# Two hybrid mixers on one core: decayed queries moved to VectorE, the triangular systems solved ahead of the index scores, gate panels fetched early, logarithms ahead of copies

## What is computed

```
n = rms_norm(h, norm_mix);  proj = n @ w_in
o_a = gated_deltanet(aq, ak, av, az, aa, ab)      # 4 heads of 128, chunks of 64
o_b = dsa_attention(bq, bk, bv, iq, ik, iw)       # index scores choose 64 of the keys per query
y = sigmoid(n @ w_gate + b_gate) gates (o_a @ w_a, o_b @ w_b);  h += y @ w_out
h += conv_gated_mlp(rms_norm(h, norm_ffn))
```

```
q, k = l2_norm(silu(conv(q))) * d**-0.5, l2_norm(silu(conv(k)))
g = -exp(a_log) * softplus(a + dt_bias);  gcum = cumsum(g);  decay = exp(gcum_i - gcum_j), i >= j
m = beta * (k k^T) * decay, strictly lower;  (m + I) [u, w] = [beta v, beta k exp(gcum)]
o = (q * exp(gcum)) S + ((q k^T) * decay) v_new     # S is the state carried from chunk to chunk
```

## Time and profile before

| | |
|---|---|
| median of three runs | 1621.33 us |
| profiled execution: its own time / its span | 1624.33 / 1622.5 us |
| TensorE matmul busy | 1583.8 us, 98% of the span |
| VectorE / ScalarE / GpSimd busy | 1178.0 (73%) / 904.1 (56%) / 71.1 us (4%) |
| mean granted TensorE clock | 0.991 |
| mixer of layer 0 / of layer 1 (from the index key's panel to the last gate panel) | 77.8 to 225 / 535 to 678 us |
| a gate load of 512 KB, from issue to landing, median | 4.4 us |

### The profile page before, as it was taken

One profiled execution on the slowest core, in us unless ns is written; L12 is line 12 of the kernel. 1 busy time (PEld: TensorE's weight loads), 2 busy tenths in 40 slices (PEclk: granted clock), 3 DMA queues, 4 the chain that ended last, 5 costly groups with the idle time before them and its releaser, 6 DMA issues.

```text
span 1622.5 us, 34719 instructions
## 1 busy us (share of the span) xinstructions
PE 1583.8 (98%) x12673; PEld 1546.3 (95%) x12673; DVE 1178.0 (73%) x1929; ACT 904.1 (56%) x1419; POOL 71.1 (4%) x62
## 2 busy tenths in 40 slices
PE   8998999999999989999999999999999999999998
PEld 7988989999999879899999989999999999999998
DVE  7778877766559689787665667888756746678863
ACT  5664565655546745656554555666545455566642
POOL 3111001000000101000000000000000000000000
PEclk9998999999999989999999999999999999999999
DMA  6633335555555432365656544566656535646553
GB/s 204 208 103 99 105 116 170 165 182 171 175 163 163 138 103 92 114 191 183 209 182 190 166 155 145 154 196 185 190 183 189 171 119 156 182 152 197 183 184 113
DMA packets 272207, 261.41 MB, mean 161 GB/s; under 512 B 20009, under 2 KB 270533, under 8 KB 272115
## 3 DMA queue, kind: packets, MB, share of 16 engines
q1 hardware_dynamic: 270547, 256.15, 50.9%
q0 software_dynamic: 1376, 3.87, 0.8%
q10 hardware_dynamic: 192, 0.14, 0.0%
HBM read 256.70 MB, written 3.42 MB: 160 GB/s over the span
## 4 chain that ended last, share of the span: by engine, by line
PE 81%; DVE 11%; ACT 4%; issue 2%; DMA 2%; SPq 1%; DVEq 0%; ACTq 0%
PE lin L551 22%; PE lin L554 22%; PE lin L559 22%; PE aux L899 5%; PE lin L899 3%; PE lin L605 3%; DVE wL L538 2%; PE lin L576 1%; ACT wH L529 1%; DVE cT L2075 1%; DMA stage<-in_w_gate 1%; DVE nT L2530 1%; DVE nT L2026 1%; DVE nL L2535 1%; PE lin L636 1%
## 5 line engine op out<-in xcount | busy, mean ns | idle before, releaser
L529 ACT ACTIVATE wH<-stage 128x1024 fp32r<-128x1024 f32 x488 | 493.7, 1049 | 481.9 <-PE lin L554 333.9
L538 DVE TENSOR_TENSOR wL<-stage,wH 128x1024 fp32r<-128x1024 f32 x488 | 580.1, 1231 | 142.2 <-PE lin L559 85.7
L551 PE MATMUL lin<-nH,wH 128*128 128x256 f32 (+2 forms) x2256 | 559.8, 287 | 1.4 <-DVE u L2579 0.7
L554 PE MATMUL lin<-nL,wH 128*128 128x256 f32 (+2 forms) x2256 | 554.7, 285 | 0.0
L551 PEld LDWEIGHTS lin<-nH,wH 128*128 128x128 f32 x2256 | 425.5, 189 | 4.7 <-issue 2.2
L554 PEld LDWEIGHTS lin<-nL,wH 128*128 128x128 f32 x2256 | 426.6, 189 | 1.1 <-issue 0.7
L559 PE MATMUL lin<-nH,wL 128*128 128x256 f32 (+2 forms) x2256 | 295.0, 283 | 0.6 <-DVE wL L538 0.6
L559 PEld LDWEIGHTS lin<-nH,wL 128*128 128x128 f32 x2256 | 281.4, 188 | 1.1 <-DVE wL L538 1.1
L551 PE MATMUL lin<-aH,wH 128*128 128x256 f32 (+1 forms) x704 | 172.3, 284 | 0.0
L554 PE MATMUL lin<-aL,wH 128*128 128x256 f32 (+1 forms) x704 | 172.2, 284 | 0.0
L551 PEld LDWEIGHTS lin<-aH,wH 128*128 128x128 f32 x704 | 132.8, 189 | 0.0
(11 more groups left out here) (416 smaller groups left out, 2202.4 us busy)
## 6 DMA issues: line engine op xcount, KB each, us to landing
stage<-in_w_up SPq DMA_DIRECT2D x88, 512.0 KB, 4.7
stage<-in_ffn_w_up SPq DMA_DIRECT2D x88, 512.0 KB, 4.1
stage<-in_w_in SPq DMA_DIRECT2D x52, 512.0 KB, 4.8
stage<-in_w_down SPq DMA_DIRECT2D x40, 512.0 KB, 3.7
stage<-in_ffn_w_down SPq DMA_DIRECT2D x40, 512.0 KB, 4.2
stage<-in_w_gate SPq DMA_DIRECT2D x32, 512.0 KB, 4.4
stage<-in_even_w_in SPq DMA_DIRECT2D x24, 512.0 KB, 4.6
stage<-in_w_out SPq DMA_DIRECT2D x16, 512.0 KB, 4.1
```

The lines of the kernel that those rows point to most:

```text
L529: nc.scalar.activation(wH[:, s, ks, 0:n], stage[:, s, ks, 0:n], ACT.Copy).then_inc(sem["whi"], 1)
L538: nc.vector.tensor_tensor(wL[:, s, ks, 0:n], stage[:, s, ks, 0:n], wH[:, s, ks, 0:n].bitcast(F32), ALU.subtract).then_inc(sem["wlo"], 1)
L551: mm = nc.tensor.matmul(banks[b][0:rows_, 0:width], wH[:, s, k, cols], xh, start=start and n == 0, stop=False)
L554: mm = nc.tensor.matmul(banks[b][0:rows_, 0:width], wH[:, s, k, cols], xl, start=False, stop=False)
```

## The change

The results are the same; the work of the two mixers is placed differently, on one engine also taken from another. VectorE's `decays(b)` is cut in two: `decay_logs(b)`, up to the release of the bank of gb, and `decays(b)`, from the wait for `dec` on. On TensorE the wait for `qe` is that of `delta_out`, on ScalarE the change of buffers is in `index_relu`, and the softplus functions moved up are those that stood behind the last norm logarithm; `w_in(6)` of ScalarE is written out so that the decay exponentials of block 2 come between its split and its copies. The diff, cut to its core:

```diff
@@ SyncE
                 gate(0, 0)
-                gate(0, 1)
                 for b in range(2):
                     kept_off(b)
+                gate(0, 1)
...
                 gate(1, 0)
+                gate(1, 1)
...
                 sp.wait_ge(sem["solved"], at("solved", l, 1))
...
                     sp.dma_start(A[b], by_token(za[b], b)).then_inc(sem["a_back"], 16)
-                gate(1, 1)
@@ GpSimd
-                    if n == 2:
-                        pool.wait_ge(sem["eg"], at("eg", l, 4))
-                        pool.wait_ge(*full("qk2", l))
-                        nc.gpsimd.tensor_tensor(cT[:, 0:4, :], cT[:, 0:4, :], eg[:, :, :], ALU.mult).then_inc(sem["qe"], 1)
@@ TensorE
-                turned("ta", iab, IDX_DIM, 16, lin_read[0])
+                turned("ta", iab, IDX_DIM, 16, (sem["iab"], at("iab", l, 1)))
...
                 index_products(1)
+                gate(0, [1])
                 pe.wait_ge(sem["sq_att"], at("sq_att", l, 1))
                 for h, name in enumerate([f"sbq{h}" for h in range(4)] + ["sbk"]):
                     mm(begin(name, l)[:, 0:T], ones, sq_att[:, h, :]).then_inc(filled(name), 1)
-                gate(0, [1])
...
-                    pe.wait_ge(sem["qe"], at("qe", l, 1))
+                    if b:
+                        pe.wait_ge(sem["qe"], at("qe", l, 1))
@@ ScalarE
+                split_hi(act, m0 + 5, 0, n=NARROW)
                 for s in range(2):
-                    split_hi(act, m0 + 5, s, n=PANEL if s else NARROW)
...
-                f(iab[IDX_DIM:NARROW, :], lin[0][IDX_DIM:NARROW, 0:T], Copy)
+                f(iab[IDX_DIM:NARROW, :], lin[0][IDX_DIM:NARROW, 0:T], Copy).then_inc(sem["iab"], 1)
+                root_log([f"ssq{h}" for h in range(4)], rnq, 1.0)
+                turned("ta", ab, 16)
+                split_hi(act, m0 + 5, 1)
+                act.wait_ge(sem["sp_in"], at("sp_in", l, 1))
+                own.done(f(gl[:, :, :], gm[:, :, :], Exp))
+                own.wait()
+                f(gl[:, :, :], gl[:, :, :], Ln, bias=one_col)
+                f(bt[:, :, :], ab[:, :, 12:16], Exp, scale=-1.0).then_inc(sem["sp_ln"], 1)
                 for p0 in (0, IDX_DIM):
                     t = f(ikr[p0:p0 + IDX_DIM, :], lin[0][0:IDX_DIM, 0:T], Copy)
...
                 f(sq_ik[:, :], ikr[:, :], Square).then_inc(sem["sq_ik"], 1)
-                root_log([f"ssq{h}" for h in range(4)], rnq, 1.0)
-                turned("ta", ab, 16)
                 root_log([f"ssk{h}" for h in range(4)], rnk, 1.0)
                 root_log(["sik"], rni, 1.0 / P)
-                act.wait_ge(sem["sp_in"], at("sp_in", l, 1))
...
-                w_in(6, lambda b: rawT[:, 16 + b:17 + b, :], slots=(0,))
+                split_hi(act, m0 + 7, 0)
                 decays(2)
+                act.wait_ge(sem["panel_done"], 2 * (m0 + 6) + 3)
+                for b in range(2):
+                    f(rawT[:, 16 + b:17 + b, :], lin[b][:, 0:T].unsqueeze(1), Copy).then_inc(lin_read[b], 1)
...
-                        if j and e < 2:
-                            act.wait_ge(sem["score"], at("score", l, e + 1))
-                        f(rl[:, e, :], bank(name)[:, :], Relu).then_inc(emptied(name), 1)
+                        if e >= 2:
+                            act.wait_ge(sem["score"], at("score", l, e - 1))
+                        f(rl[:, (2 * j + e) % 4, :], bank(name)[:, :], Relu).then_inc(emptied(name), 1)
...
                 index_relu(1)
+                gate_hi(0, [1])
                 root_log([f"sbq{h}" for h in range(4)] + ["sbk"], rnb, 1.0 / P)
                 root("sbk", rnb, 0.0)
-                gate_hi(0, [1])
@@ VectorE
                 split_lo(dve, m0 + 5, 0, NARROW)
                 times_sin(0, iq_s[:, :, :])
-                split_lo(dve, m0 + 5, 1)
                 added(0, rawT[:, 20:24, META:T], iq_s[:, :, :])
...
+                split_lo(dve, m0 + 5, 1)
...
+                decay_logs(0)
                 decays(0)
+                decay_logs(1)
                 decays(1)
...
                 keys_and_queries(1)
+                decay_logs(2)
                 times_sin(1, ik_s[:, :].unsqueeze(1))
                 decays(2)
...
                 split_lo(dve, m0 + M_GATE, 1)
+                solved()
                 index_scores(0)
-                solved()
                 gate_lo(0, [0])
                 dve.wait_ge(*read("qk2", l))
                 masked(4)
                 index_scores(1)
+                keys_decayed()
...
+                joined(4)
+                split_lo(dve, m0 + M_GATE + 1, 0)
+                masked(5)
                 take_eight(1)
-                keys_decayed()
-                split_lo(dve, m0 + M_GATE + 1, 0)
-                joined(4)
-                masked(5)
                 gate_lo(0, [1])
+                split_lo(dve, m0 + M_GATE + 1, 1)
                 dve.wait_ge(sem["att_unit"], at("att_unit", l, 3))
                 crossed(bk_s[:, :].unsqueeze(1), keys)
                 crossed(tmp4[:, :, :], queries)
-                split_lo(dve, m0 + M_GATE + 1, 1)
...
                 greatest(0)
                 biased()
+                v.tensor_tensor(cT[:, 0:4, :], cT[:, 0:4, :], eg[:, :, :], ALU.mult).then_inc(sem["qe"], 1)
                 gate_lo(2, [0])
                 normed(0)
                 state(0)
```

More of the change, by code:

```diff
@@ L211 @@
     "panel_in": 16 * M_LAYER, "whi": 4 * M_LAYER, "wlo": 4 * M_LAYER, "whi_used": 2 * M_LAYER, "panel_done": 2 * M_LAYER,
-    "lin_read": R_LAYER, "ab_in": 16,
+    "lin_read": R_LAYER, "ab_in": 16, "iab": 1,
     "sq": DC, "rstd": 2, "n": 2 * DC, "nh": DC, "nl": DC,
@@ L971, in head_squares, with turned @@
                         mm(begin(name, l)[:, 0:T], ones, sqh[:, h, :]).then_inc(filled(name), 1)
-                def turned(name, x, p0, n, free):
+                def turned(name, x, p0, n, there):
                     ps = begin(name, l)
-                    pe.wait_ge(free, r0 + 6)
+                    pe.wait_ge(*there)
                     for b in range(3):
@@ L992, in layer @@
                 t.then_inc(filled("gc"), 1)
-                turned("tv", bvT, 0, P, lin_read[3])
+                turned("tv", bvT, 0, P, (lin_read[3], r0 + 6))
                 def gate(i, slots=(0, 1)):
@@ L1558, in layer, with turned @@
                 act.wait_ge(sem["panel_done"], 2 * (m0 + 5) + 3)
-                f(iab[IDX_DIM:NARROW, :], lin[0][IDX_DIM:NARROW, 0:T], Copy)
+                f(iab[IDX_DIM:NARROW, :], lin[0][IDX_DIM:NARROW, 0:T], Copy).then_inc(sem["iab"], 1)
+                root_log([f"ssq{h}" for h in range(4)], rnq, 1.0)
+                def turned(name, to, n):
+                    act.wait_ge(*full(name, l))
+                    own.done(f(to[0:META, 0, :], bank(name)[0:META, 0:n], Copy))
+                    f(to[:, 1:3, :], bank(name)[:, n:3 * n].rearrange("p (b n) -> p b n", b=2), Copy).then_inc(emptied(name), 1)
+                turned("ta", ab, 16)
[5 more added lines that the diff above has]
+                f(bt[:, :, :], ab[:, :, 12:16], Exp, scale=-1.0).then_inc(sem["sp_ln"], 1)
                 for p0 in (0, IDX_DIM):
@@ L1565, in layer @@
                 f(sq_ik[:, :], ikr[:, :], Square).then_inc(sem["sq_ik"], 1)
-                root_log([f"ssq{h}" for h in range(4)], rnq, 1.0)
-                def turned(name, to, n):
-                    act.wait_ge(*full(name, l))
-                    own.done(f(to[0:META, 0, :], bank(name)[0:META, 0:n], Copy))
-                    f(to[:, 1:3, :], bank(name)[:, n:3 * n].rearrange("p (b n) -> p b n", b=2), Copy).then_inc(emptied(name), 1)
-                turned("ta", ab, 16)
                 root_log([f"ssk{h}" for h in range(4)], rnk, 1.0)
                 root_log(["sik"], rni, 1.0 / P)
-                act.wait_ge(sem["sp_in"], at("sp_in", l, 1))
-                own.done(f(gl[:, :, :], gm[:, :, :], Exp))
-                own.wait()
-                f(gl[:, :, :], gl[:, :, :], Ln, bias=one_col)
-                f(bt[:, :, :], ab[:, :, 12:16], Exp, scale=-1.0).then_inc(sem["sp_ln"], 1)
                 root("ssq3", rnq, lnq_col)
@@ L2151, in layer, with decay_logs @@
                 dve.wait_ge(*read("gc", l))
-                def decays(b):
+                def decay_logs(b):
                     n = TB[b][1]
@@ L2160, in decays @@
                     v.tensor_tensor(kdx[0:n, b, :], ps[0:n, n - 1:4 * n:n], gcs[0:n, b, :], ALU.subtract).then_inc(emptied(f"gb{b}"), 1)
+                def decays(b):
+                    n = TB[b][1]
                     dve.wait_ge(sem["dec"], at("dec", l, b + 1))
@@ L2214, in index_scores @@
                         for n, h in enumerate(heads):
-                            r, w = rl[:, e, n * wide:(n + 1) * wide], iw[:, j + 1, h:h + 1]
+                            r, w = rl[:, (2 * j + e) % 4, n * wide:(n + 1) * wide], iw[:, j + 1, h:h + 1]
                             if e + n == 0:
```

## The result

| | before | after |
|---|---|---|
| median, beside each other | 1621.15 us (1620.41 to 1622.37) | 1608.53 us (1607.68 to 1610.98) |
| ratio, 95% interval | | 0.9923 [0.991, 0.9935] |
| profiled execution, its time / span | 1624.33 / 1622.5 us | 1610.98 / 1609.2 us |
| mean granted clock | 0.991 | 0.994 |

The forecast was 1608.8 us, -12.5; measured were -12.6 by the medians and -13.3 by the spans.

The account below looks back on a forecast made before the run. TensorE sets the end, stalled in both mixers; with the stalls gone VectorE limits the middle. Layer 0 -0.3 - 7.9, layer 1 +3.6 - 7.9, together -12.5 us: 1608.8 us, range 1603.5 to 1614.5.

Parts of the forecast that it names:

- The early gate panel: Middle of both mixers: ScalarE's 12.39 us wait and the Y stalls of 2.4 and 3.8 us go, with their slow clock.
- The solve: Both mixers' middle: solve starts 6.0 us earlier, runs 119.6 to 127.2; X back at 133.5, its stall goes.
- VectorE is late next: Both mixers' middle: VectorE limits once the stalls go; -2.7 - 6.5 + 1.3 = -7.9 us per layer.
- rival A: Middle: TensorE, not VectorE, limits, so stalls and slow clock go whole: -20.2, in all -16.9, 1604.4 us; chance 0.17.
- The product's wait: Middle, first output: ScalarE's reading waits for VectorE's added product; TensorE loses up to 1.3 us, inside the 7.9.
- The head: Head, before panel (5,1): TensorE's hole moves to the wait for the square; layer 0 -0.3 us, layer 1 +3.6 us.
- B: Head costs nothing while the middle goes as forecast: -15.8, 1605.5 us; chance 0.10.
- C: Middle: solve waits for its gathers and holds VectorE; slower than before, chance 0.05, or 1610 to 1618 us, chance 0.06.
- D: GpSimd's rotary products block VectorE's two-input work, head holes last longer in both layers: -8.3, 1613.0 us; chance 0.10.
- The sum: Whole kernel: layer 0 -8.2, layer 1 -4.3, together -12.5 us, carried to the median: 1608.8 us.

Follow-up runs that it names:

- e5: Kernel before with only gate panel (1,1)'s load issued right behind (1,0), ahead of the wait for the solve; 1612.91 us, ratio 0.9951.
- e4: Changed kernel with the product of queries and decay back on GpSimd at its old place; 1607.14 us, ratio 0.992.
- e9: Kernel before with gate panel (1,1) loaded early and the solve ahead of block 0's index scores, nothing else; 1616.08 us, ratio 0.9975.
- again: The changed kernel, unedited, timed and profiled a second time; 1609.02 us, ratio 0.993.
- e7: Changed kernel with two of the eight search rounds for block 2's greatest scores left out; 1601.52 us, ratio 0.9884.
- e1: Changed kernel with the old head: panel (5,1)'s high halves ahead of the gates, key copies and square ahead of the logarithms; 1607.05 us, ratio 0.9921.
- e2: Changed kernel with panel (5,1)'s high halves copied at their old place, the first logarithms still ahead of the key copies; 1607.11 us, ratio 0.9921.

## Why the prediction was right, step by step

**The early gate panel.** ScalarE's 12.39 us and the Y stall went, as said; alone it gives -7.9 us (e5), its middles -10.3.

**The solve.** Forecast from 119.6 to 127.2, measured 120.10 to 127.72. X's stall went. Of the cause two things must be mended. The 2.17 us of the mask were put down to the product's move; e4 has them without it, by the subtractions' earlier place. And "ScalarE waits for the scores until about 130.5 anyhow, so nothing" dealt with later scores only; it didn't see that the swap without these edits stops ScalarE 4.67 us and TensorE 4.2 (e9). Edits priced at nothing, the norm products' place above all by the rows in e9, were a condition of the main gain.

**VectorE is late next.** Forecast per layer: enters 2.7 us earlier, saves 6.5 of 9.54 not busy, pays 1.27: -7.9. Measured on layer 0: it enters at 115.05, 2.65 earlier; 70.92 - 66.88 = 4.04 are not busy, so 5.50 saved; busy time rose by 0.32. 2.65 + 5.50 - 0.32 = 7.83. The first term was right, 1.0 too much was taken off the gaps, and 0.95 too much paid: two errors that cancel, so that the hit of this sum is in part luck. The product does cost 1.28 us, but the work that GpSimd's rotary products run over is now 0.7 us shorter in sum, the low halves by 2.3 us, while the masked products are 1.6 longer. These rows group VectorE's instructions by line, low halves and masked products, before and then after:

```profile
L538 DVE TENSOR_TENSOR wL<-stage,wH 128x1024 fp32r<-128x1024 f32 x13 | 17.6, 1397 | 0.0
...
L2179 DVE TENSOR_TENSOR ML<-MT,c 128x512 f32<-128x512 f32 x6 | 3.8, 681 | 0.0
```
```profile
L538 DVE TENSOR_TENSOR wL<-stage,wH 128x1024 fp32r<-128x1024 f32 x13 | 15.3, 1215 | 0.4 <-PE lin L559 0.4
...
L2183 DVE TENSOR_TENSOR ML<-MT,c 128x512 f32<-128x512 f32 x6 | 5.4, 933 | 0.0
```

By TensorE's stages it is -7.5 and -6.7 us (again: -7.4 and -7.4). Behind that sum stand two things of opposite sign: rival A's size, and 1.0 and 0.7 us more than its 9.4 and 10.8, up to the first new values (-10.4 and -11.5), then VectorE's bill of +2.9 and +4.8.

**The product's wait** was put at up to 1.3 us of TensorE. It was 0.6 + 0.9 and 1.7 + 0.5 us, plus the slow clock behind (3.62 instead of 1.95 us in one group): the mis-sized term in layer 1, about 1.2 us.

**The head.** Layer 0: forecast -0.3, measured -0.34 and, again, -1.74, beyond the bound of -1.2. Both are taken against the one profiled head of the kernel before, 18.02 us, which had a hole of 2.6 us and the slow clock. The same code took 15.64 us in e5, with a hole of 1.9 us and at full clock, and 17.26 in e9. Before, and then e5:

```profile
77.80:95.90 18.10, 15.41 (x97) 13.83 (x95) 12.31 (x19) 15.85 (x31) 3.40 (x1) 0.91 0.32 104
```
```profile
77.40:93.10 15.70, 13.74 (x96) 12.59 (x95) 11.83 (x19) 15.05 (x30) 3.42 (x1) 1.00 0.32 103
```

At full clock in both, the new head costs layer 0 0.6 us (16.28 against 15.64) instead of giving 0.3; that the profile showed -0.34 is luck.
Layer 1: forecast +3.6, measured +3.75 and +2.2. The chain came out, on layer 0 from 83.7 to 87.6 forecast, from 83.60 to 87.79 measured, with one link missing: the square was done at 87.27, and the bank of the last norm product was free only with the first key logarithm, at 87.65. In layer 1, 2.2 us are the chain and 1.5 the slow clock, which comes or does not. The new hole was 2.5, not 3 us.

**The rivals.** A: the limit up to the new values is TensorE, as A says, but not to the end of the stage; e7 shows what A would have given. B is refuted by e1 and e2, whose heads in layer 1 are 2.2 and 1.9 us shorter than the shorter head of the kernel after. C: the last gather was issued at 116.50 (116 forecast), with 3.6 us to the need (3.6), and no wait stands before the solve. No panel was right ahead of it: gate (0,1) had gone to the queue at 108.82. But blocks 0 and 1 were gathered right behind that panel, issued at 110.62 and 110.96. Small packets (under 512 bytes) are the gathers'. The kernel after, 110.6 to 113.1 and 113.1 to 114.1 us, then the kernel before, whose gather of block 1 was issued at 114.06 with the panel 6 us ahead, 113.7 to 114.8 and 114.8 to 115.8 us:

```profile
DMA packets 871, 0.89 MB, mean 357 GB/s; under 512 B 15, under 2 KB 870, under 8 KB 870
...
DMA packets 608, 0.13 MB, mean 126 GB/s; under 512 B 515, under 2 KB 608, under 8 KB 608
```
```profile
DMA packets 4, 0.00 MB, mean 3 GB/s; under 512 B 1, under 2 KB 4, under 8 KB 4
...
DMA packets 532, 0.03 MB, mean 34 GB/s; under 512 B 531, under 2 KB 532, under 8 KB 532
```

So a gather behind a panel just issued does wait: its packets began 2.1 us after the issue (2.0 in layer 1) instead of about 1.0. It had 6 us to spare, and this cost nothing here. D: the end's bill is a loss of D's kind, but the -7.5 and -6.7 us, or -7.4 twice, are more than its -6.5.

**The sum.** The six stages give -10.8 in the profiled execution and -14.3 in the other, around the -12.5; with the old head at full clock as the base (15.64 for 18.02) the other would give -11.9. That the median came within 0.3 us is partly luck: a range of some 2 us either way is what the clock's spells leave.

## What to carry to other kernels

When two stalls are removed, look separately at each length between fixed points: a gain of 22 us may carry a bill of 8 that a single sum hides. Before an order is swapped, name each buffer that the delayed reader holds and what stands behind its writer; an edit that looks like bookkeeping may be what the swap needs. A profile of the kernel before is one draw too: run unchanged stages again before a term of the sum is read from them. Work that one engine blocks another with can be placed where it blocks nothing: here GpSimd's product fits into VectorE's one-operand search.

## What the runs showed of the hardware

Whether the granted clock falls behind a short hole differs from one execution to the next. Seven profiled executions have the head hole of 2.49 us with the same work behind it. In layer 0 one of them has a head of 17.7 us, six of 16.28; in layer 1 five are at 17.6 to 17.9, two at 16.3. Each spell is worth 1.4 to 1.6 us, where up to 1.7 was forecast. The Trainium skill, "TensorE: Matmul & The Clock Gate", section "What's actually happening", says that the chip's look at the engine's activity runs free of the kernel and that the count of slow matmuls at a kernel's start varies by run. The traces agree in that it varies, here for holes in the middle of a kernel; that the free-running look is the reason, no run shows.

Code that no kernel here changes shows it too. A part of the second block, from 913 us in the kernel before and from 902 us in the kernel after, has the same waits (1.2, 1.1 and 0.9 us) in both; 25 us of it, before and then after:

```profile
950.00:975.00 25.00, 23.79 (x185) 22.78 (x184) 19.74 (x26) 12.22 (x24) 0.00 (x0) 0.93 0.27 87
```
```profile
939.00:964.00 25.00, 23.79 (x198) 22.78 (x198) 19.74 (x26) 12.23 (x24) 0.00 (x0) 1.00 0.27 85
```

This part is 88.52 us long before and 87.04 after: 1.5 of the 2.5 us that the changed stages don't explain. Another 0.8 lies between the layers and 0.3 elsewhere; their cause was not looked for.
